# A hybrid attention, state-space and expert block on one core: attention by pairs of heads, roots without ScalarE, state-space rounds over three units

## The reference, cut to what matters

```python
q, k = rms_norm(q, q_gain), rms_norm(k, k_gain)        # branch A: 16 heads of 64, by chunks
sc = q @ k.T * 64 ** -0.5 + bias; p = softmax(sc)      # own chunk and the ones before it
y_a = p @ v
# branch B: Mamba-2 in 4 groups: causal conv, silu, decays exp(segsum(a)), per group and 128 tokens
y_diag = ((c @ b.T) * decay) @ (x * dt); y = y_diag + y_off + d_skip * x
y_b = rms_norm(y * silu(z), per group)
# branch C: cross-attention into 256 memory tokens, 4 heads of 256, with norms of q and k
x += (sum_i sigmoid(gate_i) * (y_i @ w_br_i)) @ w_out
x += moe(rms_norm(x))                                  # top 4 of 32 experts, 3 matrices of 1024 x 1024 each
```

## Time and profile before

| | |
|---|---|
| median of 3 runs | 1508.67 us (1504.37 to 1508.69) |
| the profiled execution: time, span | 1508.17 us, 1506.1 us |
| PE busy | 1449.5 us (96%) |
| DVE, ACT, POOL busy | 605.8 (40%), 411.7 (27%), 127.9 us (8%) |
| bytes from HBM | 489.72 MB |
| mean granted PE clock | 0.99 |

### The profile page before, as it was taken

How to read it: one execution, slowest core, us unless ns; L and a number is a source line. 1 busy time by engine, 2 the same in 40 slices (tenths; PEclk the granted TensorE clock), 3 DMA queues, 4 the chain that set the end, 5 groups by cost and what they waited for, 6 DMA issues and landing times.

```text
span 1506.1 us, 18599 instructions
## 1 busy us (share of the span) xinstructions
PE 1449.5 (96%) x7575; PEld 839.1 (56%) x7575; DVE 605.8 (40%) x1130; ACT 411.7 (27%) x607; POOL 127.9 (8%) x75
## 2 busy tenths in 40 slices
PE   6999799899989999999999999999999999999998
PEld 6897578777768876444444444444444444433443
DVE  6667857888776685112112112121121121211111
ACT  5766456365545443010011011011101101101010
POOL 5112412111111210000000000000000000000000
PEclk9999899999999999999999999999999999999999
DMA  7455334444346777999999999999999999999997
GB/s 249 140 176 176 97 100 164 146 157 158 116 139 233 277 275 306 425 425 426 429 428 429 428 429 430 426 430 427 429 428 429 428 429 428 429 430 426 430 427 298
DMA packets 72656, 491.47 MB, mean 326 GB/s; under 512 B 5168, under 2 KB 7344, under 8 KB 48032
## 3 DMA queue, kind: packets, MB, share of 16 engines
q1 hardware_dynamic: 69360, 487.24, 80.0%
q10 hardware_dynamic: 2736, 3.15, 0.7%
q0 software_dynamic: 512, 0.43, 0.1%
HBM read 489.72 MB, written 1.07 MB: 326 GB/s over the span
## 4 chain that ended last, share of the span: by engine, by line
PE 77%; DMA 9%; DVE 9%; ACT 2%; issue 2%; ACTq 0%; DVEq 0%; SPq 0%
PE ps L1834 25%; PE ps L1872 12%; PE ps L1527 7%; PE ps L1762 7%; PE ps L1528 7%; PE ps L1529 7%; DMA regions<-in_w_gate 6%; PE ps L1814 4%; PE ps L1514 3%; DMA regions<-in_w_up 3%; DVE splits L998 2%; DVE regions L1101 1%; PE ps L1842 1%; DVE regions L1022 1%; PE ps L1709 1%
## 5 line engine op out<-in xcount | busy, mean ns | idle before, releaser
L1834 PE MATMUL ps<-regions,sig 128*64 128x512 f32 x2048 | 463.4, 594 | 4.1 <-DMA regions<-in_w_gate 3.9
L1834 PEld LDWEIGHTS ps<-regions,sig 128*64 128x64 f32 x2048 | 142.0, 137 | 276.6 <-issue 259.8
L1872 PE MATMUL ps<-regions,tmp 128*64 128x512 f32 x1024 | 225.1, 592 | 0.0
L1527 PE MATMUL ps<-splits,regions_r 128*128 128x512 f32 x512 | 209.0, 408 | 3.9 <-DVE regions_r L991 1.9
L1529 PE MATMUL ps<-splits,regions_r 128*128 128x512 f32 x512 | 203.2, 397 | 0.0
L1528 PE MATMUL ps<-splits,regions_r 128*128 128x512 f32 x512 | 203.2, 397 | 0.0
L710 ACT ACTIVATE splits<-halves 128x1024 fp32r<-128x1024 f32 x152 | 158.0, 1054 | 90.0 <-PE ps L1529 87.2
L998 DVE TENSOR_TENSOR splits<-halves,splits 128x1024 fp32r<-128x1024 f32 x114 | 144.8, 1277 | 54.6 <-ACT splits L710 53.6
L886 ACT ACTIVATE work<-work 128x512 f32<-128x512 f32 x32 | 20.1, 629 | 475.0 <-DVE work L1454 475.0
L1872 PEld LDWEIGHTS ps<-regions,tmp 128*64 128x64 f32 x1024 | 71.8, 137 | 131.9 <-issue 129.4
L1762 PEld LDWEIGHTS ps<-craw,regions 128*128 128x128 f32 x1024 | 119.3, 192 | 25.6 <-issue 25.2
(11 more groups left out here) (276 smaller groups left out, 1274.2 us busy)
## 6 DMA issues: line engine op xcount, KB each, us to landing
regions<-in_w_gate SPq DMA_DIRECT2D x64, 2048.0 KB, 29.2
regions<-in_w_up SPq DMA_DIRECT2D x64, 2048.0 KB, 27.6
regions<-in_w_down SPq DMA_DIRECT2D x64, 2048.0 KB, 30.4
halves<-in_w_in SPq DMA_DIRECT2D x48, 1024.0 KB, 5.2
halves<-in_w_br_b SPq DMA_DIRECT2D x8, 1024.0 KB, 5.1
halves<-in_w_mem_kv SPq DMA_DIRECT2D x8, 1024.0 KB, 5.0
halves<-in_w_br_a SPq DMA_DIRECT2D x4, 1024.0 KB, 6.4
halves<-in_w_br_c SPq DMA_DIRECT2D x4, 1024.0 KB, 5.3
```

The costliest lines, as they stand in the source:

```text
L1527: pe.matmul(out, lhs[0], rhs[0], start=start, stop=False, skip_group_check=True)
L1834: last = pe.matmul(ps[64 * h:64 * h + 64, bank, :], xgT[:, 4 * k + c], eslots[slot][:, c, h * NB:(h + 1) * NB], start=(k == 0 and c == 0), ...
L1872: last = pe.matmul(ps[64 * h:64 * h + 64, D_BANK, :], actT[:, c, 64 * k:64 * k + 64], eslots[slot][:, c, h * NB:(h + 1) * NB], start=False ...
```

## The change

The order of the blocks changes (z and k alternate, gb0 moves ahead of v, the blocks of qx ahead of bb). The state-space units follow each other every 3 weight units. Attention goes by pairs of heads over 4 units each: the scores of two heads are products over 64 rows each, from `qT` without the zeros, and the values of two heads go to the two halves of one bank in turn. Norms of q and qx are no longer multiplied into q: their inverse roots are applied to the scores. The inverse roots in the schedule come from DVE alone (`rstd_here`: a first guess from the bits, three Newton steps). Squares and sums of a norm are taken by halves. `yscale` is shared by ACT and DVE, and POOL's `clear` of `qz` goes.

```diff
-          + [("z", i) for i in range(4)] + [("k", i) for i in range(2)] + [("v", i) for i in range(2)]
-          + [("gb", 0), ("bb", 0), ("bb", 1), ("gb", 1), ("bb", 2), ("bb", 3)]
-          + [("qx", i) for i in range(2)] + [("mk", i) for i in range(2)] + [("mv", i) for i in range(2)]
-          + [("ga", 0), ("ba", 0), ("ga", 1), ("ba", 1), ("gc", 0), ("bc", 0), ("gc", 1), ("bc", 1)]
+          + [("z", 0), ("z", 1), ("k", 0), ("z", 2), ("k", 1), ("z", 3), ("gb", 0)]
+          + [("v", i) for i in range(2)] + [("qx", i) for i in range(2)]
+          + [("bb", 0), ("bb", 1), ("gb", 1), ("bb", 2), ("bb", 3), ("ga", 0)]
+          + [("mk", i) for i in range(2)] + [("mv", i) for i in range(2)]
+          + [("ba", 0), ("ga", 1), ("ba", 1), ("gc", 0), ("bc", 0), ("gc", 1), ("bc", 1)]
...
             at(w + 9, "xsT", 2 * i + 1)
     for half in range(2):
         for t in range(TT):
-            at(z0 + (5, 8)[half] + (1, 2)[half] * t, "factor", half, t)
-            at(z0 + 9 + 4 * half + t, "skip", half, t)
-        at(z0 + 11 + 4 * half, "carry", half)
+            at(z0 + (5, 12)[half] + (1, 2)[half] * t, "factor", half, t)
+            at(z0 + (9, 13)[half] + (1, 4)[half] * t, "skip", half, t)
+        at(z0 + (11, 21)[half], "carry", half)
 
     k0 = z0 + 7
-    for k in range(2 * N_UNITS + 3):
-        u, d = k // 2, k % 2
-        if u < N_UNITS:
-            if k % 4 == 0:
-                at(k0 + k, "cb", u // TT)
-            at(k0 + k, "spread", u, u // TT, u % TT, d)
-        if 1 <= k <= 2 * N_UNITS:
-            v = (k - 1) // 2
-            at(k0 + k, "weigh", v, v // TT, v % TT, (k - 1) % 2)
-        if k >= 3 and d == 1:
-            at(k0 + k, "ssm", u - 1, (u - 1) // TT, (u - 1) % TT)
-        if k >= 4 and d == 0:
-            at(k0 + k, "ysquare", u - 2, (u - 2) // TT, (u - 2) % TT)
-    ends = k0 + 2 * N_UNITS + 3
+    for u in range(N_UNITS):
+        w, of = k0 + 3 * u, (u, u // TT, u % TT)
+        if u % TT == 0:
+            at(w, "cb", u // TT)
+        for d in range(2):
+            at(w + d, "spread", *of, d)
+            at(w + 1 + d, "weigh", *of, d)
+        at(w + 3, "ssm", *of)
+        at(w + 4, "ysquare", *of)
+    ends = k0 + 3 * N_UNITS + 2
     at(ends, "ynorm")
     for t in range(TT):
-        at(ends + 1 + t, "yscale", t)
+        at(ends + 1, "yscale", t)
     for p in range(4):
-        at(ends + 4 + p, "yT", p)
-    at(ends + 8, "clear")
-    at(z0 + 5, "square", "q")
-    at(z0 + 9, "headnorm", "q")
-    for t in range(TT):
-        at(z0 + 11 + 2 * t, "headscale", "q", t)
-    at(ends + 11, "headT", "q")
-    at(ends + 1, "square", "k")
-    at(ends + 7, "headnorm", "k")
-    for t in range(TT):
-        at(ends + 8 + t, "headscale", "k", t)
-    at(ends + 12, "headT", "k")
-    def attend(w0, lo, hi):
-
-        for slot in range(hi - lo + 2):
-            for stage, m in (("scores", lo + slot), ("probsT", lo + slot - 1), ("values", lo + slot - 2),
-                             ("soften", lo + slot)):
-                if lo <= m < hi:
-                    at(w0 + 2 * slot, stage, m, *HEADS[m])
-
-    attend(ends + 14, 0, A_HEADS)
+        at(ends + 3 + p, "yT", p)
+
+    def norm_of_heads(name, squares, root, scale=()):
+
+        for t in range(TT):
+            at(squares + 2 * t, "square", name, t)
+            at(squares + 2 * t + 1, "headsum", name, t)
+        at(root, "headnorm", name)
+        for t, w in enumerate(scale):
+            at(w, "headscale", name, t)
+
+    norm_of_heads("q", z0 + 14, z0 + 19)
+    norm_of_heads("k", z0 + 21, z0 + 26, (z0 + 28, z0 + 30))
+    norm_of_heads("qx", first("ga", 0) + 1, first("ga", 0) + 6)
+    norm_of_heads("kx", first("mv", 0) + 1, first("mv", 0) + 5, (first("mv", 0) + 6, first("mv", 0) + 6))
+    for part in range(2):
+        at(ends + 7 + part, "headT", "k", part)
+        at(ends + 9 + part, "headT", "q", part)
+        at(first("mv", 0) + 2 + part, "headT", "qx", part)
+        at(first("mv", 0) + 7 + part, "headT", "kx", part)
+
+    w0 = first("bb", 0)
+    for p in range(A_HEADS // 2):
+        at(w0 + 4 * p, "scores2", p)
+        at(w0 + 4 * p + 1, "exp2", p)
+        at(w0 + 4 * p + 2, "soften2", p)
+        at(w0 + 4 * p + 3, "probsT2", p)
+        at(w0 + 4 * p + 5, "values2", p)
+    w0 = first("mv", 0) + 9
+    for slot in range(X_HEADS + 2):
+        for stage, h in (("scores", slot), ("probsT", slot - 1), ("values", slot - 2), ("soften", slot)):
+            if 0 <= h < X_HEADS:
+                at(w0 + 2 * slot, stage, A_HEADS + h, h)
     at(first("gb", 1), "memsquare")
     at(first("gb", 1) + 2, "memnorm")
     for c2 in range(4):
-        at(first("qx", 0) + 3 + c2, "memT", c2)
-    at(first("mk", 0) + 1, "square", "qx")
-    at(first("mk", 0) + 3, "headnorm", "qx")
-    for t in range(TT):
-        at(first("mk", 1) + t, "headscale", "qx", t)
-    at(first("mv", 0) + 3, "headT", "qx")
-    at(first("mv", 0) + 1, "square", "kx")
-    at(first("mv", 0) + 3, "headnorm", "kx")
-    for t in range(TT):
-        at(first("mv", 1), "headscale", "kx", t)
-    at(first("mv", 1) + 1, "headT", "kx")
-    attend(first("ga", 0), A_HEADS, A_HEADS + X_HEADS)
+        at(first("ga", 0) + c2, "memT", c2)
     at(first("bc", 1), "mergedT", 0)
     at(first("wo", 0) + 1, "mergedT", 1)
     for n in range(3):
...
-                    sp.wait_ge(misc_ready, ssm_end(N_UNITS - 1))
+                    sp.wait_ge(misc_ready, MISC_AT[("yT", 3)] + 2)
...
+                elif kind == "exp2":
+                    p = step[1]
+                    for j in range(2):
+                        h = 2 * p + j
+                        act.wait_ge(sem("maxima"), h + 1)
+                        for t, (lo, hi) in enumerate(((0, P), (P, 3 * P))):
+                            act.activation(work[:, j, lo:hi], work[:, j, lo:hi], ACT.Exp, bias=nmx[:, j, t:t + 1],
+                                           accum_out=sums[:, j, t:t + 1]).then_inc(sem("exp_out"), 1)
+                        if h + 4 < A_HEADS:
+                            load_bias(h + 4)
...
+            def rstd_here(dst, src, width):
+
+                n = dst.shape[1]
+                v, r = root_in[:, 0:n], root_out[:, 0:n]
+                link(dve.tensor_scalar(v, src, 1.0 / width, EPS, ALU.mult, ALU.add))
+                link(dve.tensor_scalar(dst.bitcast(I32), v.bitcast(I32), -0.5, RSQRT_SEED, ALU.mult, ALU.add))
+                link(dve.tensor_scalar(v, v, -0.5, None, ALU.mult))
+                for turn in range(3):
+                    link(dve.tensor_tensor(r, dst, dst, ALU.mult))
+                    link(dve.tensor_tensor(r, r, v, ALU.mult))
+                    last = dve.scalar_tensor_tensor(out=dst, in0=r, scalar=1.5, in1=dst, op0=ALU.add, op1=ALU.mult)
+                    if turn < 2:
+                        link(last)
+                return last
...
+                elif kind == "scores2":
+                    p = step[1]
+                    for j in range(2):
+                        h = 2 * p + j
+                        b = group()
+                        sc, bh = work[:, j], bias4[:, h % 4]
+                        dve.wait_ge(bias_landed[h % 4], 16 * (h // 4 + 1))
+
+                        link(dve.memset(bh[0:CHUNK, 0:CHUNK], MASKED))
+                        chain[0] += 1
+                        dve.scalar_tensor_tensor(out=sc[:, 0:P], in0=ps[:, b, 0:P], scalar=rs_q[:, h:h + 1],
+                                                 in1=backwards(bh[:, 0:P]), op0=ALU.mult, op1=ALU.add)\
+                            .then_inc(sem("vector_chain"), 1)
+                        dve.scalar_tensor_tensor(out=sc[:, P:3 * P], in0=ps[:, b, P:3 * P], scalar=rs_q[:, A_HEADS + h:A_HEADS + h + 1],
+                                                 in1=backwards(bh), op0=ALU.mult, op1=ALU.add).then_inc(misc_taken, 1)
+                        dve.wait_ge(sem("vector_chain"), chain[0])
+                        dve.wait_ge(misc_taken, misc[0])
+                        for t, (lo, hi) in enumerate(((0, P), (P, 3 * P))):
+                            chain[0] += 1
+                            dve.tensor_reduce(mx[:, t:t + 1], sc[:, lo:hi], AX, ALU.max).then_inc(sem("vector_chain"), 1)
+                        dve.wait_ge(sem("vector_chain"), chain[0])
+                        dve.tensor_scalar(nmx[:, j], mx, -1.0, None, ALU.mult).then_inc(sem("maxima"), 1)
+                        dve.wait_ge(sem("maxima"), h + 1)
...
+                elif kind == "scores2":
+                    p = step[1]
+                    banks = [group() for j in range(2)]
+                    if p == 0:
+
+                        pe.wait_ge(misc_taken, MISC_AT[("headT", "k", 1)] + 2)
+                        pe.wait_ge(misc_taken, MISC_AT[("headT", "q", 1)] + 2)
+                    for t in range(TT):
+                        for j in range(2):
+                            rows = slice(A_DIM * j, A_DIM * (j + 1))
```

(22 more changed lines are left out.)

283 lines of the change are left out of this document (139 added, 144 removed).

## The result

The kernel after takes 1488.79 us, median of 4 runs (1486.44 to 1490.34), beside 1507.72 us for the kernel before in the same session: ratio 0.9877, 95% interval 0.9855 to 0.9899. The forecast was 1474 us, 1461 to 1488. So the sign was right, and 19 of the 34 us arrived. The profiled execution took 1490.34 us; on its numbers the following stands.

A forecast was written before the change was run, and what follows sets the result against it. The prediction took PE, plus waits and slow clock, to bound the dense part, and DMA the experts after it. Gains 9.0 + 7.2 + 11.8 - 1.0 + 7.0 = 34.0 us off 1508.17 gave 1474 us, range 1461 to 1488.

The forecast's parts named there:

- The two parts in a row: Whole kernel: 579 us of dense part, then 929 us of experts; time off the first moves later loads one for one.
- no gain arrives: Rival: the stream of experts does not follow the dense part, so the time stays at 1508 us; chance 0.03.
- the slower one: Rival, attention: PE stops in every pair for a missing split, losing 5 us a pair; 1530 us, chance 0.03.
- Part 1: State-space stage: later `take z` steps remove the 7.94 us wait, the first wait stays; gain 9.0 us (3 to 19).
- Part 2: Transposes of q and k: fewer, wider DVE evictions cut the loss from 7.9 to 0.7 us; gain 7.2 us.
- Part 3: PE's work in attention: a pair of heads takes 2.53 us instead of 4.00; gain 11.8 us.
- Part 4: Waits in attention: DVE is short at three places, sum 6.0 us; loss 1.0 us more than before.
- Part 5: Norms and transposes of qx and kx: of 7.7 us lost, 0.7 stay; gain 7.0 us.
- At nothing: Taken as costing nothing: multiplies at the scores, `yscale` on two engines, fewer ACT table loads, POOL's `clear`, SP's new waits.
- The first rival: DVE bounds attention: pairs miss their 0.8 us margin when POOL's lock falls into them; 1486 us, chance 0.20.
- The rival of the row halves: Attention: products on row halves do not overlap, scores cost 1.30 us, not 0.73; 1479 us, chance 0.07.
- The one on the first wait: State-space stage: the first wait shrinks too, half of the 20.4 us of kept losses go; 1464 us, chance 0.15.

The follow-up runs named there:

- bias_late: Kernel after, with ACT's four first bias loads issued in state-space unit 3, not in the first; 1483.77 us.
- q_root_late: Kernel after, with the inverse roots of q at unit 74 instead of unit 51; 1486.18 us.
- scores_serial: Kernel after, with a pair's four score products done head after head, not in turn; 1487.83 us in one run.
- dose runs: Kernel after, with two or five extra DVE operations of 1.22 us at unit 94, in a round without a wait; 1491.86 and 1499.51 us, one run each.
- dose_two: Kernel after, with two extra DVE operations of 1.22 us at unit 94; 1491.86 us in one run.
- all_spread_more: Kernel after, with bias loads, roots of q and k, k's scalings, qx's squares and roots and branch B's last `merge` moved, memory norm split; 1465.36 us.
- roots_act: Kernel after, with the inverse roots through ACT as in the kernel before, at the places of the kernel after; 1486.27 us.
- ssm_two: Kernel after, with state-space rounds over two weight units instead of three; 1484.49 us.
- All moves together: The kernel after with all the moves of all_spread_more; 1465.36 us, ratio 0.9735 to the kernel before.

## Why the prediction was right or wrong

- **The two parts in a row** held: 18.3 us off the dense part moved the start of the experts' stream by 18.3 us, and it took 927.9 us for 927.1. That rival (no gain arrives) and the slower one are out.
- **Part 1, forecast 9.0, came to about 6.0:** units 40 to 67 take 9.5 us less, 3.5 of it the transposes of y that moved away. Over the nine traces with these steps it is 1.5 to 6.9, mostly by how long matmuls are slow. The wait of the earlier trace rows at 180 us is gone and the one at 156 us stayed, from the chain named (bias_late), 5.74 us where 6.4 were expected. Two sizes were low: its slow clock (units 42 and 43 lose 9.9 us, forecast 8.7) and the later shortages of DVE, 4.2 us at units 54 and 55 and 2.2 at 60 and 61, together 6.5 where 3.5 were taken. Behind the larger stand the roots of q, with two operations stretched beside POOL (q_root_late).
- **Part 2, forecast 7.2,** gave 7.9: no loss is left in that stretch.
- **Part 3, forecast 11.8,** gave 9.3: a clear round has 13.72 us, less four units of 2.72 is 2.84 a pair, where 2.53 was forecast and 4.00 was before. Unit 80 has 1.09 above 2.72 for scores, unit 81 1.03 for values; with 0.1 each for going back, these are 0.26 and 0.25 above the forecast terms 0.73 and 0.68; transposes took 0.2 less. So the factor of 1.8, taken from four products of 512 columns, did not carry over to score products of 128 and 256, and the order of their turns does nothing (scores_serial); the values' 0.68, taken from another product, was too low as well, for a reason that no run shows.
- **Part 4 is the step that failed:** "2.2, 2.2 and 1.6, sum 6.0", and "Loss 1.0 more than before". Measured are 5.9 us at units 88 and 89, 7.8 at 99 and 100, and 2.0 at 103 and 104: 15.7, so 10.7 more than the 5.0 of before. The places and the 3 us of room per round were right. Of the 9.7 us between 6.0 and 15.7, the waits make 4.1 (4.2, 4.2 and 1.6, sum 10.1), slow matmuls 5.2, and short gaps 0.4. Three things were left out.
  - The largest is the slow clock behind each wait, at nothing in this part though Part 1 had it: 1.7 us in all after the 4.2 at unit 88, 3.5 after the 4.2 at units 99 and 100; and 1.6 and 1.9 after 2.0 and 5.8 in the dose runs. The granted clock of the stretch was 0.96, where the kernel before had 1.00.
  - The sum at units 96 to 99: `memT` has 3.9 us of DVE, two sums of qx 2.4 and the merges 1.3, 7.6 for 3.2 of room. That is 4.4 over (PE waited 4.2), not 2.2.
  - POOL: once DVE's idle time is filled, one of its operations there takes 2.1 us longer (2.25 for 0.16 in `memnorm`, 3.29 for 1.22 at units 103 and 104 and in dose_two). `memnorm` was sized rightly at 3.8, since the 5.8 measured are 3.7 and the stretching, and so was the excess of 2.2; the 2.1 on top make the wait of 4.2. I had put the stretching at 1.7 us and left it out of the sum. A clear round escapes it only since POOL's turn falls into DVE's idle time.
- **Part 5, forecast 7.0,** gave 7.5.
- **At nothing** cost nothing in the stages looked at. In the tail, units 145 and 146 took 2.4 us more in the profiled execution than before. Six of the fourteen runs made from the kernel after have the old lengths there (5.97 to 6.02 and 2.8), the others more, so that it comes and goes between executions; whether the change makes it likelier is open.
- Sum as measured: 6.0 + 7.9 + 9.3 - 10.7 + 7.5 - 2.4 = 17.6, against 18.0 us from unit 40 to the second expert's load (18.3 less the 0.3 by which unit 40 starts earlier).
- Three slips in its sums change nothing: a pair's terms add up to 2.55, not 2.53, the chain of a pair to 8.2, not 8.3, and the losses that it keeps to 19.6, not 20.4.
- **The first rival** (DVE bounds attention, 1486 us) had the time and the resource, not the pattern: four of the eight rounds have no wait (13.7 to 13.9 us with 10.0 to 10.6 of DVE in three of them), and the loss sits where more than a pair's own work stands in a round. **The rival of the row halves** was partly right: a pair's scores cost 0.26 more than forecast, 2.1 us in all, not 0.57 and 4.6. **The one on the first wait** did not come true as built, but all_spread_more shows that its 1464 us were within reach.
- **The lock of DVE by POOL** was taken as rare, by the group of 114 rests. That row is an average over a kernel whose order mostly avoids the meeting; of the three crowded stretches of attention, two have it. The Trainium skill, SBUF — State Buffer, section Who interferes with whom, has a VectorE instruction with two SBUF inputs, and `tensor_scalar` and copies in a two-port mode, block for the whole of a GpSimd instruction that holds the ports. The runs agree: 2.25 for 0.16 us with two inputs, 2.29 and 1.83 for 0.17 and 0.18 with one, each until POOL's operation had ended.
- Parts of the change without an effect on the time that can be measured: the roots by VectorE alone (roots_act; some waits are longer by them) and the three-unit rounds (ssm_two).

## What to carry to other kernels

When a change makes the rounds of a stage shorter, add up each engine's own work for every round, with all odd steps that stand in it, and compare with the idle time of a clear round; what exceeds it is a wait in full, and the slow matmuls after it come on top; here they were more than half of what the forecast of the stage had missed. Look also at which engine's idle time hides a shared resource: once it is filled, the sharing costs as well. And when a move of one step gains nothing in the time, look at its own units and at their waits: the wait may have moved on, or the gain may be there and be hidden, since the same 2.0 us of wait made units 60 and 61 anything from 9.9 to 13.2 us long. All moves together gave 21 us here.
